# Seven products for eight in two down projections, with sums on GpSimd

## The reference

```
def swiglu_ffn(h, w_in, w_out):
    a, b = jnp.split(h @ w_in, 2, axis=-1)
    return (jax.nn.silu(a) * b) @ w_out
x = x + 0.5 * swiglu_ffn(rmsnorm(x, g), w_in, w_out)     # in the third block without the 0.5
```

## Time and profile before

| | |
|---|---|
| median of 3 runs | 2376.69 us (2375.42 to 2376.86) |
| span of the profiled execution | 2373.4 us, 30181 instructions |
| what lies around the span, against the median | 3.3 us |
| TensorE busy | 2350.3 us |
| VectorE, ScalarE, GpSimd busy | 1420.6, 1000.5, 165.1 us |
| down stages of block 2 | 1204.9 to 1264.7 and 1384.4 to 1444.3 us |
| down stages of block 3 | 2120.0 to 2180.0 and 2299.6 to 2359.7 us |

### The profile page before, as it was taken

How to read it: one execution, slowest core, us unless ns; L and a number is a source line. 1 busy time by engine, 2 the same in 40 slices (tenths; PEclk the granted TensorE clock), 3 DMA queues, 4 the chain that set the end, 5 groups by cost and what they waited for, 6 DMA issues and landing times.

```text
span 2373.4 us, 30181 instructions
## 1 busy us (share of the span) xinstructions
PE 2350.3 (99%) x11448; PEld 1971.2 (83%) x11448; DVE 1420.6 (60%) x2891; ACT 1000.5 (42%) x1852; POOL 165.1 (7%) x251
## 2 busy tenths in 40 slices
PE   9999999999999999999999999999999999999998
PEld 7888889888888888878888888888888887888887
DVE  6434546775658897875434446677754667543444
ACT  4223335442335676653322234666523346322322
POOL 0000000110001223310000000111100001000000
PEclk9999999999999999999999999999999999999999
DMA  4455434332332211223333334211223432223322
GB/s 151 118 118 142 118 111 149 116 107 81 116 102 80 73 54 63 67 89 98 98 90 107 94 108 120 81 54 58 65 83 116 132 105 67 97 88 108 98 88 90
DMA packets 86410, 231.33 MB, mean 97 GB/s; under 512 B 8505, under 2 KB 23481, under 8 KB 86267
## 3 DMA queue, kind: packets, MB, share of 16 engines
q1 hardware_dynamic: 81072, 221.42, 29.5%
q10 hardware_dynamic: 5194, 7.98, 2.1%
HBM read 217.83 MB, written 11.53 MB: 97 GB/s over the span
## 4 chain that ended last, share of the span: by engine, by line
PE 96%; DVE 2%; ACT 1%; issue 1%; DMA 0%; POOL 0%; DVEq 0%; SPq 0%; ACTq 0%
PE bank L1136 92%; PE bank L1385 2%; PE bank L1211 1%; PE bank L1557 0%; PE bank L1232 0%; DMA t_XT<-in_xT 0%; DVE t_pp L2387 0%; DVE t_pw L2387 0%; ACT t_whi L1676 0%; DVE t_PS L2120 0%; DVE t_wlo L2115 0%; DVE t_XL L2124 0%; ACT t_pw L1829 0%; DVE t_XT L2765 0%; DVE t_PW L2120 0%
## 5 line engine op out<-in xcount | busy, mean ns | idle before, releaser
L1136 PE MATMUL bank<-t_XH,t_whi 128*128 128x512 f32 x2064 | 813.4, 394 | 0.7 <-DVE t_wlo L2115 0.5
L1136 PE MATMUL bank<-t_XL,t_whi 128*128 128x512 f32 x2064 | 804.7, 390 | 0.0
L1136 PE MATMUL bank<-t_XH,t_wlo 128*128 128x512 f32 x2048 | 799.0, 390 | 0.0
L2115 DVE TENSOR_TENSOR t_wlo<-t_raw,t_whi 128x1024 fp32r<-128x1024 f32 (+2 forms) x416 | 478.6, 1152 | 386.2 <-ACT t_whi L1676 382.8
L1676 ACT ACTIVATE t_whi<-t_raw 128x1024 fp32r<-128x1024 f32 (+3 forms) x422 | 416.9, 989 | 436.8 <-PE bank L1136 371.8
L1136 PEld LDWEIGHTS bank<-t_XH,t_whi 128*128 128x128 f32 x2064 | 388.0, 188 | 80.9 <-issue 1.6
L1136 PEld LDWEIGHTS bank<-t_XL,t_whi 128*128 128x128 f32 x2064 | 388.3, 188 | 77.1
L1136 PEld LDWEIGHTS bank<-t_XH,t_wlo 128*128 128x128 f32 x2048 | 384.8, 188 | 80.9
L1136 PE MATMUL bank<-t_RX,t_whi 128*128 128x512 f32 x1056 | 325.4, 390 | 0.0
L2243 DVE TENSOR_TENSOR t_tmp<-bank,t_RB 128x512 f32<-128x512 f32 x178 | 122.6, 689 | 198.6 <-PE bank L1136 193.3
L1136 PEld LDWEIGHTS bank<-t_RX,t_whi 128*128 128x128 f32 x1056 | 198.2, 188 | 41.0 <-issue 0.2
(11 more groups left out here) (335 smaller groups left out, 2686.9 us busy)
## 6 DMA issues: line engine op xcount, KB each, us to landing
t_raw<-in_f_in SPq DMA_DIRECT2D x86, 512.0 KB, 3.5
t_raw<-in_f_out SPq DMA_DIRECT2D x32, 384.0 KB, 3.1
t_raw<-in_w_conv SPq DMA_DIRECT2D x24, 512.0 KB, 3.5
...
```

The source lines that it names most:

```text
L1136: return e.matmul(o, l, r, start=start, stop=stop, skip_group_check=True)
L2115: e.tensor_tensor(wlo[n % NRAW][:, 0:width], raw[n % NRAW][:, 0:width], f32(whi[n % NHI][:, 0:width]), ALU.subtract).then_inc(*w_lo.tick(n))
```

## The change

**The form.** In blocks 2 and 3 the product of a 2 x 2 block (two output tiles by two inner tiles; two inner tiles by two halves of 256 positions) is made of seven products instead of eight. On the weight side four parts are used as they are or in three sums more (seven in all, 7/4 of the columns); on the activation side three parts and four sums.

**Grouping.** The 22 inner tiles are worked in groups of 8, 8 and 6 (before 11 and 11), each group followed by its down products. Four output pairs (mp 0 to 3) per group; each is one `so` item per 4 inner tiles (a unit of 1024 columns; of 512 for the last 2 of group 2), in the order mp 0 and 1 first part, mp 0 and 1 second part, then mp 2, mp 3. A unit of 1024 is 42 matmuls of 256 columns. An output pair holds four banks, taken together; in the ring of 8 pairs alternate between banks 0 to 3 and 4 to 7.

**Who does what.** GpSimd makes the sums of weights (`split`, three operations in a chain, `fsum`) and of activations (`ffg`, four, `gsum`). ScalarE copies the plain and the added columns of a unit apart; VectorE subtracts both parts after GpSimd's last sum. `flo` lies in the place of `fsum`; `fhi`, `flo` have 3 buffers. `ffp` splits the activation sums of a tile pair. `merge7` puts four banks together: ScalarE copies a quarter (`P1`), VectorE does seven operations, GpSimd adds the shared sum V2 to both halves of the second output tile in groups 0 and 1; in group 2 VectorE does it in two operations. Norms of both tiles of a pair follow its merge in group 2. DMAs fetch two output tiles at once in chunks of 2 KB and less, and `raw` is free once the low parts are made.

```diff
-    ffn(1, 2, "f2_in", "f2_in", "f2_out", 0, 2 * KF, 3, [])
+    ffn_seven(1, 2, "f2_in", "f2_in", 0, 2 * KF, 3)
...
+            for mps in ((0, 1), (2,), (3,)):
+                for u in halves:
+                    for mp in mps:
+                        seven(f, g, mp, u)
+                        if late:
+                            w.add("ffp", f, g, late.pop())
+                        if u == halves[-1]:
+                            w.add("merge7", f, g, mp)
+                            if last:
+                                for m in (2 * mp, 2 * mp + 1):
+                                    norm(nxt, m)
...
 (PE) def so(f, g, mp, u, n):
+            if u == 0:
+                for z in range(4):
+                    take("f", ("so", f, g, mp, z))
...
+            for wi, xi, z, half in SEVEN:
+                o = banks[("so", f, g, mp, z)][:, 256 * half:256 * half + 256]
...
+                    done = three(o, hi[:, c], lo[:, c], ghi[j][:, x], glo[j][:, x], u == 0 and q == 0 and begins, last and q == nk - 1)
...
 (POOL) def split(n):
+            on.wait_ge(*d_raw[n % NRAW].at(n))
+            on.wait_ge(*full.at(before7(n)))
+            e.tensor_tensor(o[:, 3 * bw:5 * bw].rearrange("p (a c) -> p a c", a=2), r[:, bw:3 * bw].rearrange("p (a c) -> p a c", a=2),
+                            r[:, 3 * bw:4 * bw].unsqueeze(1).to_broadcast([P, 2, bw]), ALU.add).then_inc(*summed.tick(("two", n)))
+            on.wait_ge(*summed.at(("two", n)))
+            e.tensor_tensor(o[:, 5 * bw:6 * bw], o[:, 4 * bw:5 * bw], r[:, bw:2 * bw], ALU.add).then_inc(*summed.tick(("three", n)))
+            on.wait_ge(*summed.at(("three", n)))
+            e.tensor_tensor(o[:, 6 * bw:7 * bw], o[:, 5 * bw:6 * bw], r[:, 0:bw], ALU.add).then_inc(*summed.tick(("four", n)))
...
 (DVE) def split(n):
+                on.wait_ge(*summed.at(("four", n)))
+                on.wait_ge(*w_hi.at((n, 0)))
+                e.tensor_tensor(flo[i][:, plain], r[:, plain], f32(fhi[i][:, plain]), ALU.subtract).then_inc(*w_lo.tick((n, 0)))
+                on.wait_ge(*w_hi.at(n))
+                e.tensor_tensor(flo[i][:, added], fsum[i][:, added], f32(fhi[i][:, added]), ALU.subtract).then_inc(*w_lo.tick(n))
...
 (DVE) def merge7(f, g, mp):
+            e.tensor_tensor(U2, b0[:, 256:512], P1, ALU.subtract).then_inc(*evac.tick(("u2", *item)))
+            if g:
+                on.wait_ge(*summed.at(("x7", f, g - 1, mp)))
+            e.tensor_tensor(x1[:, 0:256], x1[:, 0:256], P1, ALU.add).then_inc(*evac.tick(("x11", *item), ("free", ("so", *item, 0))))
...
+            e.tensor_tensor(V2, b1[:, 0:256], U2, ALU.add).then_inc(*evac.tick(("v2", *item), ("free", ("so", *item, 1))))
+            e.tensor_tensor(U2, b3[:, 256:512], U2, ALU.add).then_inc(*evac.tick(("u4", *item)))
...
+            e.tensor_tensor(x1[:, 256:512], x1[:, 256:512], U2, ALU.subtract).then_inc(*evac.tick(("x12", *item)))
+            e.tensor_tensor(x2, x2, b3, ALU.add).then_inc(*evac.tick(("x2", *item), ("free", ("so", *item, 3))))
...
+            on.wait_ge(*full.at(("so", *item)))
+            on.wait_ge(*evac.at(("x12", *item)))
+            e.tensor_tensor(x1, x1, b2, ALU.add).then_inc(*evac.tick(("free", ("so", *item, 2)), *([("xt", nxt, 2 * mp)] if last else [])))
...
 (POOL) def merge7(f, g, mp):
+            on.wait_ge(*evac.at(("x2", f, g, mp)))
+            e.tensor_tensor(x2, x2, V2.unsqueeze(1).to_broadcast([P, 2, 256]), ALU.add).then_inc(*summed.tick(("x7", f, g, mp)))
```

More of the change, by code:

```diff
@@ L450, in ffn, with seven, ffn_seven @@
                         w.add("spill", f, m)
-                elif f == 1 and m == 0:
-                    w.add("winload")
+    def seven(f, g, mp, u):
+        size = GROUPS[g][1]
+        k, n = GROUPS[g][0] + 4 * u, 4 if 4 * u + 4 <= size else 2
+        i = w.unit(("f2_out", "fd")[f - 1], (mp, k, n), 2 * n * P)
+        w.seven.append(i)
+        w.add_units("so", (f, g, mp, u), [i])
+    def ffn_seven(f, ni, wa, wb, oa, ob, nxt):
+        for g, (start, size) in enumerate(GROUPS):
+            pairs, late = PAIRS[size], []
+            for m in range(size):
+                first = g == 0 and m == 0
+                if first and ni in EACH:
+                    n, n2 = w.unit(wa, oa), w.unit(wb, ob)
+                    w.both = 1
+                    w.add_units("pair", (f,), [n, n2])
+                    for k in range(KD):
+                        w.add("normsq", ni, k)
+                    w.both = 0
+                    continue
+                second = g == 0 and m == 1 and ni in EACH
+                w.lin("ffa", f, g, m, name=wa, j=oa + start + m)
+                if late:
+                    w.add("ffp", f, g, late.pop())
+                if first or second:
+                    w.add("nstat", ni)
+                w.lin("ffb", f, g, m, name=wb, j=ob + start + m)
+                if first or second:
+                    w.add("nspread", ni)
+                if second:
+                    w.add("ffg", f, g, 0)
+                w.add("ffg", f, g, m)
+                late += [j for j, p in enumerate(pairs) if p[1] == m]
+            last = g == len(GROUPS) - 1
+            halves = range((size + 3) // 4)
+            for mps in ((0, 1), (2,), (3,)):
+                for u in halves:
+                    for mp in mps:
+                        seven(f, g, mp, u)
+                        if late:
+                            w.add("ffp", f, g, late.pop())
+                        if u == halves[-1]:
[3 more added lines that the diff above has]
+                                    norm(nxt, m)
+                                    if f == 2:
+                                        w.add("gain", m)
+                                    if f < 2:
+                                        w.add("spill", f, m)
+            if f == 1 and g == 0:
+                w.add("winload")
@@ L1127, in norm_r, with before7, x7 @@
         return rn[:, 8 * ni:8 * ni + 4], rn[:, 8 * ni + 4:8 * ni + 8]
+    place7 = {n: i for i, n in enumerate(w.seven)}
+    def before7(n):
+        i = place7[n] - NSEVEN
+        return ("u", w.seven[i]) if i >= 0 else ("ffa", 1, 0, 0)
+    def x7(i, q=0, n=1):
+        return slice(i * 256 + q * P, i * 256 + q * P + n * P)
     NT = {("n", i): 4 for i in range(7)}
@@ L1156, in weights @@
             on.wait_ge(*w_lo.at(n))
+            if n in place7:
+                return fhi[place7[n] % NSEVEN], flo[place7[n] % NSEVEN]
             return whi[n % NHI], wlo[n % NRAW]
@@ L1296, in ffo, with so @@
             dense(("ffo", f, h, m), n2, GH, GL, ("g", f, h), nk=5, k0=6, first=False)
+        def so(f, g, mp, u, n):
+            last = 4 * u + 4 >= GROUPS[g][1]
+            if u == 0:
+                for z in range(4):
+                    take("f", ("so", f, g, mp, z))
+            hi, lo = weights(n)
+            nk = unit[n][2] // (4 * P)
+            for q in range(nk):
+                operand(("gp", f, g, 2 * u + q))
+            for wi, xi, z, half in SEVEN:
+                o = banks[("so", f, g, mp, z)][:, 256 * half:256 * half + 256]
+                begins = wi in (A1, AC, D_, B)
+                for q in range(nk):
+                    c = slice((wi * nk + q) * P, (wi * nk + q + 1) * P)
+                    x = slice(256 * xi, 256 * xi + 256)
+                    j = 2 * u + q
+                    done = three(o, hi[:, c], lo[:, c], ghi[j][:, x], glo[j][:, x], u == 0 and q == 0 and begins, last and q == nk - 1)
+                if last and wi in (ACD, CD):
+                    done.then_inc(*full.tick(("so0" if wi == ACD else "so1", f, g, mp)))
+            done.then_inc(*full.tick(("u", n), *([("so", f, g, mp)] if last else [])))
         def conv(m, part, n):
@@ L2101, in act_program, with spot7, waits7 @@
                 do[kind](*args)
+    def spot7(g, m):
+        return next((j, p.index(m)) for j, p in enumerate(PAIRS[GROUPS[g][1]]) if m in p)
+    def waits7(f, g, m):
+        if m >= 4:
+            return [(f, g, m - 4)]
+        return [(f, g - 1, m + 4)] if g else []
     def dve_program(e):
@@ L2829, in final @@
                 e.tensor_tensor(XT[:, 7, :], XT[:, 7, :], RB, ALU.mult).then_inc(*scaled.tick(("final", 7)))
[L2831 to L2832 removed]
+        do = dict(widestat=widestat, winload=winload, final=final, cclear=cclear, scale=scale, hidzero=hidzero, sparsezero=sparsezero,
+                  ffg=ffg, merge7=merge7)
+        n = 2
+        for (kind, *args), upto in w.items:
+            while n < min(upto - 1 + NHI, len(unit)):
+                if n in place7:
+                    split(n)
+                n += 1
             if kind in do:
```

143 lines of the change are left out of this document (131 added, 12 removed).

## The result

The changed kernel takes 2471.51 us (median of 4 runs, 2470.63 to 2472.19) against 2376.78 for the one before on the same chip: ratio 1.0397, 95% interval 1.0383 to 1.0412, 94.7 us slower. Forecast were 2440 and a range up to 2470. The direction held; the size was a third too small (+63.0 against +94.7). The profiled span is 2469.7 us against 2373.4, +96.3.

What follows compares the result with a forecast made beforehand. TensorE was taken to bound the kernel; 18.0 us saved there against stalls of 40.8 in block 2 and 40.2 in block 3 gave +63.0, so span 2436.4 and median 2439.7 us (2440). The range was 2398 to 2470.

Steps and rivals of the forecast that it cites:

- Direction and bound: Whole kernel: TensorE bounds it before; the change makes it slower (chance 0.90), since the other engines hold TensorE up.
- Matmul saving: Down products on TensorE: 924 matmuls of 256 columns replace 528 of 512, saving 9.0 us per block, 18.0 in all.
- Sum of idle time: TensorE's waits in blocks 2 and 3: 10.9 us per group of 8, 19.0 and 18.4 for the two group 2s.
- Pair 3 of the groups of 8: Seventh unit (g) of a group of 8: its weights come late, so TensorE waits 5.9 us.
- The lock: GpSimd's sums and VectorE's splits exclude each other by alternation; a group of 8 loses 10.9 us, 3.6 without it.
- The rival without its weight: GpSimd's sums slip into VectorE's pauses, so exclusion costs nothing: +29.2 us, 2406; chance 0.22.
- The heavier GpSimd path: GpSimd's sums with a broadcast operand half as slow again, +0.6 us per unit: +24, 2464; chance 0.15.
- The first unit's wait for the last ffb bank: Start of a group: TensorE's first unit waits up to 1.0 us, counted as covered by the third unit's wait.
- c's own wait: Third unit of a group of 8: waits for the pair operand's split and starts 3.8 us late.
- T0: Time origin of the hand-walked order: end of a group's last ffb; the units after it are lettered a to h.
- Weight loads, priced at nothing: Weight DMAs: 3.1 us to landing, asked for at least 6 us ahead; some 1 us per group if cover went.
- The rival on the faster side: Stalls under 9.0 us per block decide: 12 us gained, 2365; chance 0.08.

Runs made afterwards that it cites:

- e1: Changed kernel with dummy 512-column matmuls put where TensorE waited, ahead of first units and of output pair 3's first unit: 2462.05 us, ratio 1.0357.
- e2: Changed kernel with GpSimd's three weight sums per unit replaced by memsets of about the same length and the same waits: 2444.07 us, ratio 1.028.
- e12: Changed kernel with plain group 2, reordered group start and weight sums on VectorE, but every second unit's sums given back to GpSimd: 2391.14 us, ratio 1.0062.
- e9: Kernel before the change, with TensorE made to stand still eight times, 4.72 us each, while GpSimd clears columns: 2436.95 us, ratio 1.0255.
- e4: Changed kernel with a group's last inner tile ahead of the second unit's split, and GpSimd's shared merge sum behind the next unit's weight sums: 2445.93 us.
- e3: Changed kernel with the weight sums left out altogether, ScalarE and VectorE taking the added columns from raw: 2402.17 us, ratio 1.0106.
- e7: Changed kernel with weight sums on VectorE, last inner tile first and GpSimd's shared merge sum behind the next unit's weight sums: 2436.12 us, ratio 1.025.

## Why the prediction was right in direction and wrong in size

- **Direction and bound: right.** TensorE bound before, and every stage of the form waits for the others now.
- **Matmul saving: right.** 0.120 us each at full clock; 18.0 us in all.
- **Sum of idle time: right as a sum, in part by luck.** Forecast 81.0 (4 x 10.9 + 19.0 + 18.4); measured 69.4 in the stages, 2.0 at the mixer's first product, 2.4 at 1952 and 3.3 in the tail, 77.1. The slow clock hid a part of the waits, as e1 shows. Group 2's idle times are at both places named: 5.7 for banks (forecast 6.6), 3.7 and 3.3 at pair 3 (6.0). Pair 3 of the groups of 8: 5.0 (5.9).
- **The lock: right.** 1514 for 1231, alternating, 27 us of the weight sums alone. The rival without its weight (2406) falls; e2 and e12 show it from both sides. The heavier GpSimd path falls too: its sum of 512 columns with a repeated operand takes 1.29 us with VectorE idle (at 1169.03), as the plain one of the earlier trace rows.
- **The first step that failed: the clock, for which the sum has no term.** It priced each idle time at its own length and every matmul at 0.120 us. Around each idle time of 3.3 to 7.0 us the clock fell to 1.2 GHz for 3.4 or 6.8 us: 70.4 us of matmuls in all ran at it beyond the 3.4 of the kernel before, nominally 35 us. The kernel before has no idle time in these stages and no fall there; e9 shows that an idle time of 4.7 costs 7.1 where nothing else is late. With it, 77.1 + 35.2 - 18.0 = 94.3, against 94.7.
- **The second step that failed: GpSimd's queue at the first unit.** "The first unit's wait for the last ffb bank (up to 1.0) falls before c's own wait and is covered by it." It is 5.1 to 6.5 in three groups of four. My walk over GpSimd's queue began with the last pair's four sums, and left out that the four of tile 6 stand ahead of the sums of a and b, and that VectorE reads `ffa`'s bank only behind split b. So its premise that "VectorE's two steps end at T0 + 1.7" was wrong: the last of them (L2445) ends 7.0 to 7.1 us behind T0 in all four groups of 8 (1182.08 in the first, with T0 at 1175.03), and GpSimd's last four activation sums begin that much later. e4, which moves this work ahead of split b, shortens the first wait to 3.1 to 4.5. The wait at the first unit hid the one at c (3.8 forecast, 0.9 and 0.2 found; where the first wait is short, as in block 3's group 0, c has 7.0). At full clock a group of 8 loses 14.5, by e1, and not 10.9.
- **How much each is worth.** On the span 33.3 us were missed (+63.0 against +96.3). The groups of 8 have 22.4 of them (227.2 against 4 x 51.2): e1 leaves 14.6, which I put down to the queue, and takes away 7.8, which is the clock's alone. Block 3's group 2 and its tail have 5.3 (17.2 + 6.5 against 18.4), the wait at 1952 2.4 and the stretches at 933 and 1028 2.9. Block 2's group 2 was right (16.7 and 2.0 behind it, against 19.0). The shares are of this order only, since clock and queue cover each other: half of the slow matmuls' loss came back as idle time when the clock was held up.
- **Weight loads, priced at nothing: right for the groups of 8,** by e3.
- **The rival on the faster side** asked for stalls under 9.0 per block. Its counter-argument, throughput of VectorE in group 2, holds: group 2 costs 41.5 us of the 94.7, and in e7 VectorE alone works 44.2 us in it.

Nothing tried beats the kernel before. With sums on VectorE a group of 8 has 42.7 to 44.4 us of VectorE for 43.5 of TensorE in the plain form, and with sums on GpSimd the lock makes it longer. A gain would need a third place for the sums, or fewer of them; no run shows one.
